# Row halves transposed in two steps, and a last row block that ends on 256 columns

## The reference

```python
# first block, for each of 2 layers
proj = x @ w_in[l]                          # 8200 columns: retention, mLSTM, gates
mix  = (gate_a * y_ret + gate_b * y_ml) @ w_out[l]
x = _layer_norm(DEEPNORM_ALPHA * x + mix, ln1_g[l], ln1_b[l])
gu = x @ w_gate_up[l]
hidden = jax.nn.silu(gu[..., :D_FF]) * gu[..., D_FF:]
x = _layer_norm(DEEPNORM_ALPHA * x + hidden @ w_down[l], ln2_g[l], ln2_b[l])
# second block, for each of 2 layers
proj = rms_norm(x, norm_gain) @ w_in        # dilated attention, RG-LRU, stick-breaking attention
x = x + y @ w_out
# at the end: rms_norm(h, final_gain), that is xf * rsqrt(mean(xf * xf) + 1e-6) * gain
```

## Time and profile before

| | |
|---|---|
| median of 3 runs | 1176.04 us (1175.67 to 1177.94) |
| the profiled execution: own time | 1177.04 us |
| its span in the trace | 1175.2 us, so 1.84 us lie around it |
| PE busy | 1158.7 us, 99% |
| DVE, ACT busy | 747.7 and 570.4 us, 64% and 49% |
| mean granted TensorE clock | 0.995 |

### The profile page before, as it was taken

One profiled execution on the slowest core, in us unless ns is written; L12 is line 12 of the kernel. 1 busy time (PEld: TensorE's weight loads), 2 busy tenths in 40 slices (PEclk: granted clock), 3 DMA queues, 4 the chain that ended last, 5 costly groups with the idle time before them and its releaser, 6 DMA issues.

```text
span 1175.2 us, 18028 instructions
## 1 busy us (share of the span) xinstructions
PE 1158.7 (99%) x7546; PEld 1042.8 (89%) x7546; DVE 747.7 (64%) x1006; ACT 570.4 (49%) x658; POOL 26.2 (2%) x36
## 2 busy tenths in 40 slices
PE   8999999999999999999999999999999899999997
PEld 6988998998999988998998898899988689978996
DVE  4867557667655546686764667755545667875775
ACT  5563445442544434454544534444432466755664
POOL 0000000001000000000000000000000100000000
PEclk9999999999999999999999999999999999999999
DMA  9664454556666463745446556665566353437330
GB/s 340 224 215 144 144 183 176 182 186 199 225 213 191 165 212 115 250 146 177 160 143 200 169 190 215 223 202 183 183 197 215 125 203 124 141 123 263 113 104 36
DMA packets 129871, 211.45 MB, mean 180 GB/s; under 512 B 6528, under 2 KB 52608, under 8 KB 129664
## 3 DMA queue, kind: packets, MB, share of 16 engines
q1 hardware_dynamic: 128048, 204.02, 52.1%
q0 software_dynamic: 1744, 6.29, 1.9%
HBM read 209.24 MB, written 1.05 MB: 179 GB/s over the span
## 4 chain that ended last, share of the span: by engine, by line
PE 92%; DVE 3%; ACT 3%; issue 1%; DMA 0%; POOL 0%; SPq 0%; DVEq 0%; POOLq 0%; ACTq 0%
PE ps L470 88%; PE ps L663 1%; DVE wl L1372 1%; ACT wh L947 1%; PE ps L698 1%; PE ps L603 1%; ACT sg L1110 0%; DMA rv<-in_w_in 0%; PE ps L801 0%; DVE sg L1652 0%; PE ps L670 0%; PE ps L783 0%; DVE xl L1458 0%; ACT xh L983 0%; DVE X L1631 0%
## 5 line engine op out<-in xcount | busy, mean ns | idle before, releaser
L1372 DVE TENSOR_TENSOR wl<-raw,wh 128x2048 fp32r<-128x2048 f32 (+1 forms) x190 | 424.1, 2238 | 175.6 <-ACT wh L947 175.2
L947 ACT ACTIVATE wh<-raw 128x2048 fp32r<-128x2048 f32 (+1 forms) x190 | 359.9, 1900 | 181.7 <-PE ps L470 166.9
L470 PE MATMUL ps<-xh,wh 128*128 128x256 f32 x1200 | 337.3, 282 | 0.0
L470 PE MATMUL ps<-xl,wh 128*128 128x256 f32 x1200 | 332.3, 277 | 0.0
L470 PE MATMUL ps<-xh,wl 128*128 128x256 f32 x1184 | 328.5, 277 | 0.0
L470 PEld LDWEIGHTS ps<-xh,wh 128*128 128x128 f32 x1200 | 225.9, 188 | 3.2 <-issue 2.4
L470 PEld LDWEIGHTS ps<-xl,wh 128*128 128x128 f32 x1200 | 225.9, 188 | 0.4
L470 PEld LDWEIGHTS ps<-xh,wl 128*128 128x128 f32 x1184 | 222.7, 188 | 0.0
L470 PE MATMUL ps<-wh,xh 128*128 128x512 f32 (+1 forms) x512 | 203.9, 398 | 4.9 <-DVE wl L1372 2.7
L470 PE MATMUL ps<-wl,xh 128*128 128x512 f32 (+1 forms) x512 | 197.3, 385 | 0.0
L470 PE MATMUL ps<-wh,xl 128*128 128x512 f32 (+1 forms) x512 | 197.2, 385 | 0.0
(11 more groups left out here) (269 smaller groups left out, 1394.5 us busy)
## 6 DMA issues: line engine op xcount, KB each, us to landing
raw<-in_w_in SPq DMA_DIRECT2D x90, 1024.0 KB, 5.0
raw<-in_w_gate_up SPq DMA_DIRECT2D x88, 512.0 KB, 4.8
raw<-in_w_down SPq DMA_DIRECT2D x20, 1024.0 KB, 5.0
raw<-in_w_out SPq DMA_DIRECT2D x16, 1024.0 KB, 5.0
raw<-in_w_proj_ret SPq DMA_DIRECT2D x8, 1024.0 KB, 4.9
raw<-in_w_proj_mlstm SPq DMA_DIRECT2D x8, 1024.0 KB, 4.9
rows<-in_ln_g POOLq DMA_DIRECT2D x4, 512.0 KB, 4.4
rows<-in_ln_b POOLq DMA_DIRECT2D x4, 512.0 KB, 6.0
```

What stands on the lines that cost most here:

```text
L470: return pe.matmul(o, a, b, start=start, stop=False, skip_group_check=True)
L947: act.activation(stretch(wh, u, 0, m), source(u)[:, 0:m], ACT.Copy).then_inc(s_hi, 1)
L1372: dve.tensor_tensor(stretch(wl, u, a, nk * n), source(u)[:, a:nk * n], f32(stretch(wh, u, a, nk * n)), ALU.subtract).then_inc(s_lo, 1 if a ...
```

## The change

It has three parts.

1. **Two steps.** `turn_x` now turns one column half q per call, and `half_k` calls `mid` in front of two k-steps, `mid_at` and the one behind it. `by_half` has `mid_at` = 2 as its only value. In the three turns of token half 0 (`out1` twice, `dn1` of layer 0) q = 0 moves from kk = 3 to kk = 2, q = 1 stays at kk = 3. In the five turns of token half 1 (all pairs) q = 0 stays at kk = 2 and q = 1 moves to kk = 3. `dn1` of layer 1 and the turn inside `project` keep both halves together.
2. **Shared squares.** In `mean_square`, which now ends five of the six row halves, ACT squares only columns 0 to 511 (with a scale of 1/32, so that the sum is already divided by 1024), and DVE squares columns 512 to 1023 with a running sum that starts at epsilon; one DVE addition is left.
3. **The last rows** (t = 1 of the last layer). Columns 768 to 1023 of `o1` get a bank of their own, `e`; the 24 matmuls of `o1` become 48 on 256 columns. The last k-steps (k = 4 to 7) run as all of `o0`, then the left part of `o1`, then the right. `last_rows` replaces `mean_square` on DVE with squares cut the same way, and ACT scales columns 0 to 511.

```diff
         "V2", "c0", "c1", "T6", "T7", "c2", "c3", "V3", "l0", "l1", "k0", "k1", "k2", "k3", "p0", "p1",
-        "x00", "x01", "x10", "x11")
+        "x00", "x01", "x10", "x11", "e")
 SIDE1 = {
...
         f32 = lambda ap: ap.bitcast(F32)
+        end_of_all = lambda l, t: l == DEPTH - 1 and t == 1
         flat = lambda a: a[:, :, :].rearrange("p k t -> p (k t)")
...
                 for c in range(2):
-                    sp.wait_ge(s_rm, 4 * 2 + 2 * t + c + 1)
+                    if t == 1 and c == 0:
+                        sp.wait_ge(s_last, 2)
+                    else:
+                        sp.wait_ge(s_rm, 4 * 2 + 2 * t + c + (t == 0))
                     sp.dma_start(out[P * t:P * t + P, col_half(c)], xn(t)[:, col_half(c)]).then_inc(s_out, 16)
...
                 for kk in range(nk):
-                    if mid and kk == mid_at:
-                        mid()
+                    if mid and kk - mid_at in (0, 1):
+                        mid(kk - mid_at)
                     if t == 0 and kk in (0, nk // 2):
...
                     r.then_inc(s_half, 1)
+                if mid and mid_at == nk - 1:
+                    mid(1)
 
-            def by_half(name, l, head, tail, lh, ll, ready, mid, mid_at=3):
+            def by_half(name, l, head, tail, lh, ll, ready, mid, mid_at=2):
                 k = 0
...
 
-            def turn_x(l, tag, t, v, src, seen):
-                for q in range(2):
-                    name = f"{tag}{t}{q}"
-                    bank, fill = open_aux(name, l)
-                    pe.wait_ge(seen, v + 2 * t + q + 1)
-                    for g in range(4):
-                        r = pe.transpose(bank[:, tok_half(g)], src[:, P * (4 * q + g):P * (4 * q + g) + P], ident)
-                    r.then_inc(fill, 1)
+            def turn_x(l, tag, t, v, src, seen, q):
+                bank, fill = open_aux(f"{tag}{t}{q}", l)
+                pe.wait_ge(seen, v + 2 * t + q + 1)
+                for g in range(4):
+                    r = pe.transpose(bank[:, tok_half(g)], src[:, P * (4 * q + g):P * (4 * q + g) + P], ident)
+                r.then_inc(fill, 1)
 
...
                 one("out0", mxh, mxl, mix_ready(l), "tok")
-                by_half("out1", l, 0, 2, mxh, mxl, mix_ready(l), lambda: turn_x(l, "xa", 0, 8 * l, X[:, 0, :], s_xn))
-                pair("ff0", "ff1", l, x_part(2 * l + 1), lambda: turn_x(l, "xa", 1, 8 * l, X[:, 1, :], s_xn),
+                by_half("out1", l, 0, 2, mxh, mxl, mix_ready(l), lambda q: turn_x(l, "xa", 0, 8 * l, X[:, 0, :], s_xn, q))
+                pair("ff0", "ff1", l, x_part(2 * l + 1), lambda q: turn_x(l, "xa", 1, 8 * l, X[:, 1, :], s_xn, q),
                      lambda: hidden_turn(l, 0, 0), lambda: hidden_turn(l, 0, 1))
...
                 if l == 0:
-                    by_half("dn1", l, 4, 2, hdh, hdl, hidden_ready(l), lambda: turn_x(0, "xb", 0, 4, X[:, 0, :], s_xn), 3)
+                    by_half("dn1", l, 4, 2, hdh, hdl, hidden_ready(l), lambda q: turn_x(0, "xb", 0, 4, X[:, 0, :], s_xn, q))
                 else:
-                    by_half("dn1", l, 3, 3, hdh, hdl, hidden_ready(l), lambda: turn_x(1, "xb", 0, 0, xn(0), s_rm), 2)
+                    by_half("dn1", l, 3, 3, hdh, hdl, hidden_ready(l), lambda q: [turn_x(1, "xb", 0, 0, xn(0), s_rm, n) for n in range(2) if q == 0])
 
...
                         for t in range(2):
-                            r = tok3(bank[t][:, :], yh, yl, k, t, h_[:, k, :], l_[:, k, :], k == 0)
+                            if end_of_all(l, t) and c == 1:
+                                if k == 0:
+                                    rest, _ = open_aux("2e", l)
+                                tok3(bank[t][:, 0:256], yh, yl, k, t, h_[:, k, 0:256], l_[:, k, 0:256], k == 0)
+                                r = tok3(rest[:, 0:256], yh, yl, k, t, h_[:, k, 256:512], l_[:, k, 256:512], k == 0)
+                            else:
+                                r = tok3(bank[t][:, :], yh, yl, k, t, h_[:, k, :], l_[:, k, :], k == 0)
                         if k == 3:
...
                 for t in range(2):
+                    if end_of_all(l, t):
+                        ends = (0, 0, 512, main("o0", l)[1], s_used), (1, 0, 256, main("o1", l)[1], s_used), (1, 256, 512, *aux("2e", l)[:2])
+                        for c, a, z, o, full in ends:
+                            u, nk, h_, l_ = last[c]
+                            for k in range(4, 8):
+                                r = tok3(o[:, 0:z - a], yh, yl, k, t, h_[:, k - 4, a:z], l_[:, k - 4, a:z], False)
+                            r.then_inc(full, 1)
+                        continue
                     for k0 in (6, 4):
...
 
-            def squares(t, v, waits):
-                for c in range(2):
-                    act.wait_ge(*waits[c])
-                    r = act.activation(xn(t)[:, col_half(c)], X[:, t, col_half(c)], ACT.Square, accum_out=st6[:, t, c, 0:1])
-                r.then_inc(s_sq, 1)
+            def squares(t, ready, value, rest):
+                act.wait_ge(ready, value)
+                act.activation(rest, X[:, t, 0:512], ACT.Square, scale=D ** -0.5, accum_out=st6[:, t, 0, 0:1]).then_inc(s_sq, 1)
 
...
                         highs(use + RING)
-                    waits = [(freed(f"o{c}", l, t)[0], freed(f"o{c}", l, t)[1] + 1) for c in range(2)]
-                    squares(t, 5 + l, waits)
+                    free, v = freed("o0", l, t)
+                    squares(t, free, v + 1, flat(xc) if end_of_all(l, t) else xn(t)[:, 0:512])
+                    if end_of_all(l, t):
+                        act.wait_ge(s_last, 1)
+                        act.wait_ge(s_rms, 6)
+                        act.activation(xn(t)[:, 0:512], xn(t)[:, 0:512], ACT.Copy, scale=rsd[:, t:t + 1]).then_inc(s_last, 1)
 
...
 
-            def mean_square(t, n):
+            def square_sum(x_, start_, sum_):
+                return dve.tensor_tensor_reduce(x_[0], x_[1], x_[1], 1.0 / D, start_, ALU.mult, ALU.add, sum_)
+
+            def mean_square(t, n, x_ready):
+                x_ready()
+                after(own(square_sum((xn(t)[:, 512:1024], X[:, t, 512:1024]), RMS_EPS, rsd[:, t:t + 1])))
                 dve.wait_ge(s_sq, n)
-                after(own(dve.tensor_tensor(rsd[:, t:t + 1], st6[:, t, 0, 0:1], st6[:, t, 1, 0:1], ALU.add)))
-                dve.tensor_scalar(rsd[:, t:t + 1], rsd[:, t:t + 1], 1.0 / D, RMS_EPS, ALU.mult, ALU.add).then_inc(s_ms, 1)
+                dve.tensor_tensor(rsd[:, t:t + 1], st6[:, t, 0, 0:1], rsd[:, t:t + 1], ALU.add).then_inc(s_ms, 1)
                 dve.wait_ge(s_row2, 16 * ((n + 1) // 2))
...
 
+            def last_rows(l):
+                o, x_, gain, bank = xn(1), X[:, 1, :], rows2, main("o1", l)[1]
+                residual(l, "o0", 1, 0, 1.0)
+                main_done("o0", l, 1)
+                dve.wait_ge(s_row2, 48)
+                dve.tensor_tensor(o[:, 0:512], x_[:, 0:512], gain[:, 0:512], ALU.mult).then_inc(s_last, 1)
+                main_full("o1", l, 1)
+                after(own(dve.tensor_tensor(x_[:, 512:768], x_[:, 512:768], bank[:, 0:256], ALU.add)))
+                n = own(square_sum((o[:, 768:1024], x_[:, 512:768]), RMS_EPS, rsd[:, 1:2]))
+                own(dve.tensor_tensor(o[:, 512:768], x_[:, 512:768], gain[:, 512:768], ALU.mult))
+                after(n)
+                dve.wait_ge(s_sq, 6)
+                own(dve.tensor_tensor(st6[:, 1, 1, 0:1], st6[:, 1, 0, 0:1], rsd[:, 1:2], ALU.add))
+                rest, _ = aux_full("2e", l)
+                after(own(dve.tensor_tensor(x_[:, 768:1024], x_[:, 768:1024], rest[:, 0:256], ALU.add)))
+                square_sum((o[:, 768:1024], x_[:, 768:1024]), st6[:, 1, 1, 0:1], rsd[:, 1:2]).then_inc(s_ms, 1)
+                dve.wait_ge(s_rms, 6)
+                dve.tensor_scalar(o[:, 512:768], o[:, 512:768], rsd[:, 1:2], None, ALU.mult)
+                dve.scalar_tensor_tensor(out=o[:, 768:1024], in0=x_[:, 768:1024], scalar=rsd[:, 1:2], in1=gain[:, 768:1024],
+                                         op0=ALU.mult, op1=ALU.mult).then_inc(s_rm, 1)
+
             def normal(l, name, t, a, eps, n):
...
                 if n == 4:
-                    mean_square(t, t + 1)
+                    mean_square(t, t + 1, lambda: dve.wait_ge(s_xn, 12 + 2 * t + 2))
 
...
                         raise_high(use + RING)
+                    if end_of_all(l, t):
+                        last_rows(l)
+                        continue
                     for c in range(2):
...
                         first_half_low()
-                    mean_square(t, 2 * l + 2 + t + 1)
+                    mean_square(t, 2 * l + 2 + t + 1, lambda: main_done(f"o1", l, t))
 
```

14 lines of the change are left out of this document (7 added, 7 removed).

## The result

The changed kernel takes 1181.77 us (median of 22 runs, 1174.71 to 1185.06), the kernel before 1175.79 us (22 runs, 1174.14 to 1179.48) beside it. The ratio is 1.0043, 95% interval 1.0035 to 1.0052: slower by about half a per cent. The forecast was 1174.8 us with a range up to 1176.8, and "slower by over 0.2%" had a chance of 6%. The time lies above the range, and the case that came true is the one with 6%.

What follows compares the result with a forecast made beforehand. PE, 92% of the chain that ended last, was taken as the bound; 0.7 - 0.2 + 0.5 + 0.25 = 1.25 us gained, so 1175.8 us profiled and 1174.8 us median, range 1172.7 to 1176.8.

Steps and rivals of the forecast that it cites:

- slower by over 0.2%: Whole kernel: a time over 1178.4 us, given a chance of 0.06.
- the first durations' paragraph: Durations used throughout: four transposes 0.44 us, 256-column matmul pitch 0.118 us, 512-column 0.231 us; splitting 24 costs 0.1 to 0.3 us.
- the rivals: Second piece not late 15%, low clock gone 14%, another low stretch 11%, no gain from the turns 12%; forecast itself 48%.
- Part 1, turns of token half 0: First block's three turns: transposing q = 0 one k-step earlier gains 0.48 of PE's 0.60 us idle time each.
- The pairs behind them: Pairs of token half 1 behind those turns: DVE's piece becomes late, leaving 0.23 us each, 0.7 us gained in all.
- the turns give nothing: First-block turns: ACT or DVE's piece takes all the gain back; sum 0.6 us, time 1175.4 us; chance 12%.
- Layer 0: Second block, shared squares: 0.42 us gained, uncovered transposes at half clock cost 0.6; 0.2 us lost (bounds 0 and 0.5).
- Layer 1: Second block, shared squares: DVE's square fits its idle time at token half 1; 0.5 us gained (bounds 0.2 and 0.8).
- Part 3: Last rows: scaling starts as before, shorter scalings and earlier stores gain 0.25 us (bounds 0.3 lost, 0.5 gained).
- Its lower case: Last rows: the second store lands only 0.1 us earlier if both stores share the engines' rate, against 0.4 otherwise.
- Sum without the pitch: All edited places: 0.7 - 0.2 + 0.5 + 0.25 = 1.25 us gained.
- the low clock goes: Second block, layer 0, behind 929.90: the half-clock stretch vanishes, worth 1.2 us; sum 2.45 us, time 1173.6 us; chance 14%.

Runs made afterwards that it cites:

- The turns of token half 0 alone: The kernel before with only the three turns of token half 0 in two steps; 1173.70 us, ratio 0.9979.
- the fast variant: The changed kernel with only the turns inside the pairs (token half 1) in one step again; 1171.99 us, ratio 0.9960.
- Its two short executions: The changed kernel unchanged, profiled twice more on one chip; 1174.79 and 1177.56 us.
- its six repetitions: The changed kernel unchanged, once more in rounds beside the kernel before; 1181.44 us, ratio 1.0046.
- part 1 alone: The kernel before with every turn of TensorE in two steps, squares and last rows as before; 1177.13 us, ratio 1.0007.

## Why the prediction was wrong

**The failed step is the first durations' paragraph.** It took "A 256-column matmul has a pitch of 2.83/24 = 0.118 us" from one row and let it stand for the kernel. The sum then had terms for the edited places alone: the time of the matmuls that the change leaves as they are was put at nothing gained or lost, without a reason, and none of the rivals let PE's own stream change its pace. The trace of before held both: the 24 matmuls at 213 us are at the long pitch, the long stretch at 309 us at the short one. 1630 matmuls at the one or the other are 7.2 us, nearly six times the whole forecast gain. The executions above show that this term, and no wait, makes the changed kernel slower: its spans are 1178.9 and 1180.8 us with both stretches at the long pitch, and 1172.9 and 1175.5 with both at the short one, a little below the kernel before.

**Part 1, turns of token half 0.** The mechanism was right, and so was its size: 0.48 us forecast, 0.46 to 0.54 measured.

**The pairs behind them.** Forecast was a net gain of 0.23 us for each. Between executions of equal clock the turn gives -0.52, -0.48 and -0.56 and the pair behind it takes back 0.49, 0.47 and 0.49: 0.1 to 0.2 us in all and not 0.7. The forecast let DVE's piece move 0.2 us forward; it did not move, and the second four transposes are fully uncovered. This was the rival "the turns give nothing", at 12%.

**Part 2.** Layer 0: forecast 0.2 lost. Measured about nothing at full clock (-0.22 and +0.25) and 0.5 lost where the clock fell (-0.19, +0.13 and +0.53). The forecast was made for the half clock; there the loss is at its bound of 0.5. Layer 1: forecast 0.5 gained, measured 0.50 (0.23 + 0.11 + 0.16).

**Part 3.** Forecast 0.25 gained, measured 0.06. Its lower case, 0.1 if both stores share the rate, came true, as the packets show.

**Sum without the pitch:** 1.25 forecast, 0.7 measured at full clock and 0.3 where the clock fell.

**The clock.** By the profiled execution after, "the low clock goes" (14%) came true. But the changed kernel has the fall at the `q`, `k` turn in two of its other executions and the kernel before lacks it in one. The turns of token half 0 alone even had one behind the turn in `project` instead (window, length, busy by engine, clock):

```profile
1042.00:1045.00 3.00, 3.00 (x10) 2.45 (x10) 1.98 (x3) 2.75 (x3) 0.00 (x0) 0.53 0.05 18
```

For this change it is a matter of the execution, some 1.3 us each on the average: every profiled execution with a mean granted clock of 0.997 or lower has such a fall, and so low are 17 of 28 runs of the changed kernel and 48 of 71 of the kernel before, a like share. It should have been a part of the range and not a rival of the change. The order of the work is not without influence, though: of the 11 runs of the fast variant, with the new last rows or the old ones, none is that low. A part of its gain is the falls that it lacks; why it lacks them is not shown.

**What stays open.** What in the hardware holds the pitch is not shown. Breaks select it, and two patterns of starts of the 512-column matmuls ahead of `ff2` go with the two outcomes (with two breaks in `ff2`, the distances of starts behind the pair's last break begin with about 314, 235, 233 ns ahead of each short stretch, and with 317, 224, 231 or 313, 231, 231 ahead of each long one; this holds for all 36 such stretches of the traces). So by all that the traces show, the pair's turn acts by the phase in which it leaves the stream. Why the changed kernel leaves the other phase in most executions and not in all isn't settled, and my one rule for it failed. Its two short executions were on another chip than its six repetitions, so the chip is not excluded as a part of it; two of its first 22 runs, at 1174.71 and 1175.91 us beside others of 1178.20 and more, speak for a difference between executions too. Nor is it known why part 1 alone, with the same order on TensorE, has the long pitch less often.

## What to carry over

Measure the pitch of every long stretch of matmuls in the profile, by the distances of their starts, before pricing an edit, and ask whether it is the best one that the same trace shows; a difference of 4% there was worth 3.6 us a layer, more than all waits that this change removes, and an edit ahead of it can change it. A wait that is hidden behind transposes is hidden by all of them: where another engine is late, splitting the cover costs what the split part took. Compare single executions only at equal pitch and equal clock, and repeat them.

## What the hardware showed

- At a granted clock of 1.00 and with PE never idle, the stream of weight load and 256-column matmul runs at 113.4 or 117.8 ns a matmul, and holds that over up to 815 matmuls (92 to 96 us). The records of single matmuls are 276 ns long at the one and 281 ns at the other, without scatter:

```profile
L470 PE MATMUL ps<-xl,wh x213: 276/276/276, 329.7 to 401.8; 128*128 128x256 f32 x107
```

```profile
L474 PE MATMUL ps<-xl,wh x210: 281/281/281, 329.9 to 403.7; 128*128 128x256 f32 x105
```

- Of the breaks seen, those of two transposes sometimes change the pitch, to the short one or back; those of four transposes at `om` and in `ff2` left the long one in place each time (in `ff2` they were met in one of the two phases only).
- The granted clock fell to 0.50 for 3.4 us early on and at the `q`, `k` turn of layer 0, or nowhere, in executions of the same code (kernel before and changed kernel), and in one other kernel behind the turn in `project`.
